# Attention scores of a fused transformer block: fp32 products against three fp32r passes on high and low parts

## The chip, the cores and the metric

One core of a Trainium2 chip runs the whole program: two model blocks in one launch, three mixers and three feed-forward networks, on 512 tokens of width 1024. The metric is the device time of that core in microseconds. TensorE is the matrix engine (PE in the profile, its weight loads PEld), VectorE is DVE, ScalarE is ACT, GpSimd is POOL, and SyncE issues most DMAs.

## The reference

Only the first mixer matters here, the dilated attention of `first_block`. There are 12 heads of 64, and every query looks at three dilated windows:

```python
q, k = rope(q, pos), rope(k, pos)
attn_out = dilated_attention(q, k, v).reshape(B, S, ATTN_WIDTH)

def dilated_branch(q, k, v, window, dilation):     # (128, 1), (512, 4), (2048, 16)
    ...
    s = jnp.einsum('brnqhd,brnkhd->brnhqk', qs.astype(jnp.float32), kb.astype(jnp.float32)) * scale
    s = jnp.where(valid[None, None, :, None], s, -jnp.inf)
    m = jnp.max(s, axis=-1, keepdims=True)
    e = jnp.exp(s - m)
    ...
    o = jnp.einsum('brnhqk,brnkhd->brnqhd', e / den, vb.astype(jnp.float32))
```

The kernel computes each causal score once per head and folds the three windows into one additive table (BIAS: 8 times the logarithm of the number of windows that see the key), so the scores of a head are 512 queries against the keys up to the query's block of 128. `rope` multiplies by cosines and adds the swapped halves times sines.

## The kernel before, in words

Activations lie transposed: features on the 128 partitions, 512 tokens along the row. Every projection is an output tile of 128 features, called a unit, and is computed as three fp32r passes: weights high times input high, high times low (line 394 and 395, `high_part`), and low times high (line 403, `low_part`). ScalarE makes the high part of the weights (a copy to fp32r, line 375), GpSimd the low part (weights minus high part, `split_lo`, line 647, both inputs in SBUF), and it starts on a unit as soon as the high part is there and the buffer's last unit has ended.

The attention takes the 12 heads as 6 pairs, one pair to a tile of 128 partitions: head h=0 on rows 0 to 63, head h=1 on rows 64 to 127. The code of each engine is a function `attn_stage(j, a)`: stage j projects queries, keys and values of pair j (units u, u+1, u+2) while it does scores, softmax and values of pair a = j - 1. The stages run j = 0 to 5, and then one with the last pair's attention alone. The order of each engine's work is written out by hand, and semaphores join the engines.

TensorE, stage j (lines 1033 to 1131): `scores` of pair a (line 1052); `turn_v` (1092); query unit into bank B[0]; `values` of pair a - 1 (1083); key unit into B[1]; `turn(0)`, ten transposes of head 0's probabilities (1068); a wait for the queries (`a_qk`, line 1128), since the value unit reuses B[0]; the high part of the value unit; `turn(1)`, which waits until VectorE has copied head 0's transposes out; its low part; in stages 2 and 4 one product of the pooling branch (1031). The next stage's `scores` wait for the keys (`a_qk`), and for both engines' copies of the turned probabilities (`a_pt_act`, `a_pt_dve`), because they reuse those banks.

The scores are 8 fp32 products, 4 per head, of widths 512, 384, 256 and 128 keys. Each contracts only 64 rows, so the two heads' products occupy different halves of the array. The profile shows an fp32 product as two matmul records, so 16 records per stage.

VectorE, stage j (2670 to 2775): `mask` and row maxima (2716), `normalise` (2725 to 2729), and for n = 0 (queries) and 1 (keys) `times_cos(n)` (2680), then, after ScalarE has copied the four swapped quarters (`swap_halves`, 1886), `rotate(n)`: times sine (2684), wait, and the add into QT1 or KT1 (2688, tiles QT and KT in the trace). In stages 2, 3 and 4 the window sums of the pooling branch (2650) stand between `rotate(0)` and `times_cos(1)`; stages 2 and 4 have its averages (2665) before `rotate(1)` and its differences (2668) after it. `copy_probs(0)` comes before `rotate(1)` and `copy_probs(1)` after it (2736, 2738); `scale_v` (2694) is last.

QT1 and KT1 are two buffers each in turns over the stages (index j % 2), fp32.

Of the kernel before, what the change touches and what calls it, by code (L numbers as in the profile page):

```python
# [19 lines left out]
P = 128  # L20
T = 512
D = 1024
DC = D // P
# [17 lines left out]
ALU = mybir.AluOpType  # L41
ACT = mybir.ActivationFunctionType
F32 = mybir.dt.float32
F32R = mybir.dt.float32r
# [43 lines left out]
def s_width(block):  # L88
    return P * (block + 1)
# [46 lines left out]
def build(nc, ins, out_t):  # L136
    ctx = ExitStack()
    with ctx:
# [6 lines left out]
        def sem(name):  # L145
            return ctx.enter_context(nc.semaphore(name))

        def scratch(tensors):

            with ExitStack() as stack:  # L150
                return [alloc(stack, *t) for t in tensors]
# [65 lines left out]
        def back(u):  # L217
# [3 lines left out]
        pad = 16  # L221
        (M1H, M1L, QT1, KT1, VN1, QC, RT, PR, PT, BIAS, CS1, SN1, V1, MX, NM, DEN, RD,
         UP, WA, WB, INV, DF, YT, WPOOL) = scratch([
             ("M1H", [P, DC, T], F32R), ("M1L", [P, DC, T], F32R), ("QT1", [P, 2, T]), ("KT1", [P, 2, T]),
             ("VN1", [P, 2, TB, P]), ("QC", [P, 2, T]), ("RT", [P, 2, T]), ("PR", [P, 2, WIDE]),
             ("PT", [P, 2, WIDE]), ("BIAS", [P, T]), ("CS1", [P, T]), ("SN1", [P, T]),
             ("V1", [P, T]), ("MX", [P, 2, TB]), ("NM", [P, 2, TB]), ("DEN", [P, 2, TB]), ("RD", [P, 2, TB]),
# [49 lines left out]
        B = [ctx.enter_context(nc.psum_tensor(f"B{n}", [P, T], F32)) for n in range(8)]  # L277
# [189 lines left out]
        a_cos = sem("a_qk_times_cosine")  # L467
        a_swapped = sem("a_qk_halves_swapped")
        a_sin = sem("a_qk_times_sine")
        a_qk = sem("a_qk_ready")  # L470
        a_vs = sem("a_v_scaled")
        a_vt = sem("a_v_turned")
        a_v = sem("a_v_ready")
        a_scores = sem("a_scores_ready")
# [234 lines left out]
        def _(pe):  # L709
# [323 lines left out]
            def attn_stage(j, a):  # L1033
# [4 lines left out]
                ap = None if a is None else a % 2  # L1038

                def scores():  # L1040

                    pe.wait_ge(a_qk, a * 2 + 2)
                    if not first_a:
                        pe.wait_ge(a_pt_act, a * 2)
                        pe.wait_ge(a_pt_dve, a * 4)
                    for h, tb, bank, at in ((0, 1, 4, 0), (1, 3, 5, 0), (0, 3, 2, 0), (1, 2, 6, 0), (0, 2, 3, 0),
                                            (1, 1, 4, 256), (0, 0, 3, 384), (1, 0, 6, 384)):
                        w = s_width(tb)
                        r = slice(64 * h, 64 * h + 64)
                        if h == 1 and bank == 4:  # L1050
                            pe.wait_ge(a_scores, a * 8 + 1)
                        pe.matmul(B[bank][:, at:at + w], QT1[r, ap, P * tb:P * tb + P], KT1[r, ap, 0:w],  # L1052
                                  start=True, stop=True).then_inc(a_scores, 1)

                def turn(h):
                    hd = a * 2 + h
# [38 lines left out]
                if a is not None:  # L1095
                    scores()
                    turn_v()
# [1083 lines left out]
        def _(dve):  # L2181
# [488 lines left out]
            def attn_stage(j, a):  # L2670
# [3 lines left out]
                jp = None if j is None else j % 2  # L2674
# [7 lines left out]
                def rotate(n):  # L2682
                    dve.wait_ge(a_swapped, j * 8 + 4 * n + 4)
                    dve.tensor_tensor(RT[:, 1, :], QC[:, n, :], SN1[:], ALU.mult).then_inc(a_sin, 1)
                    dve.wait_ge(a_sin, j * 2 + n + 1)
                    if j >= 2:
                        dve.wait_ge(a_scores, j * 8 - 8)
                    dve.tensor_tensor((QT1, KT1)[n][:, jp, :], RT[:, 0, :], RT[:, 1, :], ALU.add).then_inc(a_qk, 1)  # L2688

                def scale_v():  # L2690
                    wait_unit(dve, u + 2)
# [56 lines left out]
                if j is not None:  # L2748
                    rotate(0)
                    if a is not None and a - 1 in POOL_ENDS:  # L2750
                        pool_lo(POOL_ENDS[a - 1])
# [10 lines left out]
                if j is not None:  # L2762
                    if first:
                        take_pools()
                    if a in POOL_ENDS:
                        pool_averages(POOL_ENDS[a])
                    rotate(1)
                    if a in POOL_ENDS:
                        pool_differences(POOL_ENDS[a])
# [389 lines left out]
```

## Time and profile before

| | |
|---|---|
| median of 3 runs | 1915.99 us (1915.64 to 1916.06) |
| profiled execution, device time | 1915.55 us |
| its span, first to last instruction | 1913.8 us |
| mean granted TensorE clock | 1.000 |
| PE busy | 1907.8 us, 100% of the span |
| DVE busy | 1157.4 us, 60% |
| ACT busy | 886.8 us, 46% |
| POOL busy | 469.4 us, 25% |
| scores of the first mixer (line 1052) | 96 matmul records, from 37.5 to 159.4 us |

Busy time of an engine is the union of its instructions. A matmul's record is longer than the time it occupies the array, because consecutive ones overlap: the distance from one start to the next is what a matmul costs in a stream. A VectorE record overlaps the one before it by some 0.08 us where nothing holds it up.

### The profile page before, as it was taken

Reading aid. Unit: us, or ns where it says so; the run is one execution under the profiler, and the core shown is the slowest. Engines: PE = TensorE matmul, PEld = TensorE weight load, DVE = VectorE, ACT = ScalarE, POOL = GpSimd, SP = SyncE. Lnnn points to the kernel's source line nnn. Section 1 sums busy time; section 2 is a strip of 40 time slices with the busy share of each in tenths; the row PEclk is TensorE's granted clock in tenths of the full one; section 3 lists DMA queues with packets and bytes.
Section 4 is the critical chain, followed back from the end, with each engine's and each line's share of the span. In section 5 each row is a group of like instructions: output and inputs, shape, how many; then the busy total and the mean of one; then the engine's idle time right before and its main releaser. Section 6 shows DMA issues by size and latency. Waiting matters only on the chain.

```text
span 1913.8 us, 29035 instructions
## 1 busy us (share of the span) xinstructions
PE 1907.8 (100%) x10235; PEld 1617.4 (85%) x10235; DVE 1157.4 (60%) x1685; ACT 886.8 (46%) x1386; POOL 469.4 (25%) x181
## 2 busy tenths in 40 slices
PE   9999999999999999999999999999999999999999
PEld 6777889998888888888889999888777788999887
DVE  5775688866237455464277876423777778787500
ACT  6665544445234434434254444424767554444421
POOL 3323300003423343343420000443322240000243
PEclk9999999999999999999999999999999999999999
DMA  5222233223223232232333222332212132232232
GB/s 177 66 67 78 67 126 117 99 77 106 95 85 106 71 99 82 71 101 74 99 101 131 99 99 76 104 99 78 72 60 66 55 113 97 101 113 93 91 106 89
DMA packets 48889, 177.41 MB, mean 93 GB/s; under 512 B 5552, under 2 KB 6448, under 8 KB 48816
## 3 DMA queue, kind: packets, MB, share of 16 engines
q1 hardware_dynamic: 36864, 137.29, 22.1%
q10 hardware_dynamic: 11952, 39.13, 5.8%
q8 instruction: 47, 0.77, 0.2%
q14 instruction: 26, 0.21, 0.0%
HBM read 174.30 MB, written 2.10 MB: 92 GB/s over the span
## 4 chain that ended last, share of the span: by engine, by line
PE 98%; DVE 1%; ACT 0%; issue 0%; DMA 0%; SPq 0%; DVEq 0%; ACTq 0%
PE B L394 20%; PE B L395 20%; PE B L403 20%; PE B L870 6%; PE B L866 6%; PE B L868 6%; PE B L1224 1%; PE B L415 1%; PE B L1228 1%; PE B L1225 1%; PE B L420 1%; PE B L416 1%; PE B L1405 1%; PE B L1442 1%; PE B L1428 1%; PE B L1052 1%
## 5 line engine op out<-in xcount | busy, mean ns | idle before, releaser
L647 POOL TENSOR_TENSOR WL<-RAW,WH 128x1024 fp32r<-128x1024 f32 (+1 forms) x170 | 458.4, 2699 | 1418.9 <-ACT WH L375 854.8
L375 ACT CAST WH<-RAW 128x1024 fp32r<-128x1024 f32 (+1 forms) x232 | 258.4, 1115 | 444.1 <-PE B L395 358.2
L394 PE MATMUL B<-HH,WH 128*128 128x512 f32 x1064 | 418.9, 394 | 0.3 <-DVE QT L2688 0.3
L395 PE MATMUL B<-HL,WH 128*128 128x512 f32 x1064 | 415.4, 390 | 0.0
L403 PE MATMUL B<-HH,WL 128*128 128x512 f32 x1064 | 265.1, 391 | 0.0
L394 PEld LDWEIGHTS B<-HH,WH 128*128 128x128 f32 x1064 | 200.0, 188 | 42.2 <-issue 1.7
L395 PEld LDWEIGHTS B<-HL,WH 128*128 128x128 f32 x1064 | 200.1, 188 | 39.8
L403 PEld LDWEIGHTS B<-HH,WL 128*128 128x128 f32 x1064 | 196.8, 188 | 40.0 <-POOL WL L647 0.4
L395 PE MATMUL B<-ML,WH 128*128 128x512 f32 x440 | 171.3, 389 | 0.0
L394 PE MATMUL B<-MH,WH 128*128 128x512 f32 x440 | 171.3, 389 | 0.0
L870 PE MATMUL B<-TH,SL 128*128 128x256 f32 x544 | 153.0, 281 | 0.0
L866 PE MATMUL B<-TH,SH 128*128 128x256 f32 x544 | 153.0, 281 | 0.0
L868 PE MATMUL B<-TL,SH 128*128 128x256 f32 x544 | 152.9, 281 | 0.0
L1586 ACT CAST SH<-SUMS 128x512 fp32r<-128x512 f32 (+1 forms) x102 | 77.9, 765 | 135.5 <-DVE SUMS L2283 95.4
L2194 DVE TENSOR_TENSOR ACC<-ACC,SQ 128x512 f32<-128x512 f32 x38 | 74.6, 1964 | 107.9 <-ACT SQ L1531 107.8
L2474 DVE TENSOR_TENSOR X<-X,B 128x512 f32 x26 | 17.9, 687 | 198.8 <-PE B L403 193.2
L870 PE MATMUL B<-HH,SL 128*128 128x256 f32 x408 | 114.8, 281 | 0.0
L866 PE MATMUL B<-HH,SH 128*128 128x256 f32 x408 | 114.8, 281 | 0.0
L868 PE MATMUL B<-HL,SH 128*128 128x256 f32 x408 | 114.8, 281 | 0.0
L868 PEld LDWEIGHTS B<-TL,SH 128*128 128x128 f32 x544 | 104.3, 192 | 2.5
L866 PEld LDWEIGHTS B<-TH,SH 128*128 128x128 f32 x544 | 102.2, 188 | 2.6
L403 PE MATMUL B<-MH,WL 128*128 128x512 f32 x429 | 103.6, 389 | 0.0
(430 smaller groups left out, 3622.8 us busy)
## 6 DMA issues: line engine op xcount, KB each, us to landing
RAW<-in_w_small SPq DMA_DIRECT2D x186, 512.0 KB, 3.5
RAW<-in_w_large SPq DMA_DIRECT2D x48, 704.0 KB, 4.1
SUMS<-in_w_seven ACTq DMA_DIRECT2D x34, 512.0 KB, 3.6
R<-in_w_seven ACTq DMA_DIRECT2D x17, 512.0 KB, 4.4
HD<-in_w_seven ACTq DMA_DIRECT2D x17, 512.0 KB, 4.4
out_t<-X SPq DMA_DIRECT2D x7, 256.0 KB, 5.2
X<-in_x_t ACTq DMA_DIRECT2D x4, 256.0 KB, 6.3
X<-in_x_t SPq DMA_DIRECT2D x4, 256.0 KB, 6.6
```

The source lines that it names most:

```text
L375: act.copy(wh, raw).then_inc(s_hi, 1)
L394: pe.matmul(bank, wh[:, c, :], xh[:, k0 + c, :], start=(start and c == 0), stop=False)
L395: mm = pe.matmul(bank, wh[:, c, :], xl[:, k0 + c, :], start=False, stop=False)
L403: mm = pe.matmul(bank, wl[:, c, :], xh[:, k0 + c, :], start=False, stop=(stop and c == chunks - 1))
L415: pe.matmul(bank, wh[:, c, :], xh[:, k0 + c, :], start=(start and c == 0), stop=False)
L416: pe.matmul(bank, wh[:, c, :], xl[:, k0 + c, :], start=False, stop=False)
L647: pool.tensor_tensor(wl, raw, wh.bitcast(F32), ALU.subtract).then_inc(s_lo, 1)
L866: pe.matmul(bank, wh, xh[:, rows.start + c, cols], start=(start and c == 0), stop=False, skip_group_check=True)
L868: pe.matmul(bank, wh, xl[:, rows.start + c, cols], start=False, stop=False, skip_group_check=True)
L870: mm = pe.matmul(bank, wl, xh[:, rows.start + c, cols], start=False, stop=(c == 3), skip_group_check=True)
L1586: act.copy(SH7[:, form, :], src).then_inc(t_hi, 1)
L2194: dve.tensor_tensor(ACC[:], ACC[:], SQ[b][:], ALU.add).then_inc(s_sq_used, 1)
```

## The change

The scores are computed as three fp32r passes in place of fp32: query high times key high, query low times key high, query high times key low. The products are issued in four twos, one of each head, and within a two pass by pass. QT1 and KT1 become fp32r, and their two halves now hold the high and the low part of one pair in place of two pairs in turns, so that VectorE waits for all scores of the pair before (`a_scores`) before it writes them. `rotate(n)` gets two more VectorE operations: the add is done twice, once rounded to fp32r (the high part) and once in fp32 (into RT), and after a wait for both the difference is the low part.

```diff
-             ("M1H", [P, DC, T], F32R), ("M1L", [P, DC, T], F32R), ("QT1", [P, 2, T]), ("KT1", [P, 2, T]),
+             ("M1H", [P, DC, T], F32R), ("M1L", [P, DC, T], F32R), ("QT1", [P, 2, T], F32R), ("KT1", [P, 2, T], F32R),
...
-                    for h, tb, bank, at in ((0, 1, 4, 0), (1, 3, 5, 0), (0, 3, 2, 0), (1, 2, 6, 0), (0, 2, 3, 0),
-                                            (1, 1, 4, 256), (0, 0, 3, 384), (1, 0, 6, 384)):
-                        w = s_width(tb)
-                        r = slice(64 * h, 64 * h + 64)
-                        if h == 1 and bank == 4:
-                            pe.wait_ge(a_scores, a * 8 + 1)
-                        pe.matmul(B[bank][:, at:at + w], QT1[r, ap, P * tb:P * tb + P], KT1[r, ap, 0:w],
-                                  start=True, stop=True).then_inc(a_scores, 1)
+                    for two in (((0, 1, 4, 0), (1, 3, 5, 0)), ((0, 3, 2, 0), (1, 2, 6, 0)),
+                                ((0, 2, 3, 0), (1, 1, 4, 256)), ((0, 0, 3, 384), (1, 0, 6, 384))):
+                        for n, (q, k) in enumerate(((0, 0), (1, 0), (0, 1))):
+                            for h, tb, bank, at in two:
+                                w = s_width(tb)
+                                r = slice(64 * h, 64 * h + 64)
+                                if n == 0 and h == 1 and bank == 4:
+                                    pe.wait_ge(a_scores, a * 8 + 1)
+                                mm = pe.matmul(B[bank][:, at:at + w], QT1[r, q, P * tb:P * tb + P], KT1[r, k, 0:w],
+                                               start=(n == 0), stop=(n == 2), skip_group_check=True)
+                                if n == 2:
+                                    mm.then_inc(a_scores, 1)
...
-                    if j >= 2:
-                        dve.wait_ge(a_scores, j * 8 - 8)
-                    dve.tensor_tensor((QT1, KT1)[n][:, jp, :], RT[:, 0, :], RT[:, 1, :], ALU.add).then_inc(a_qk, 1)
+                    if j:
+                        dve.wait_ge(a_scores, j * 8)
+                    hi, lo = ((QT1, KT1)[n][:, part, :] for part in range(2))
+                    dve.tensor_tensor(hi, RT[:, 0, :], RT[:, 1, :], ALU.add).then_inc(a_hi, 1)
+                    dve.tensor_tensor(RT[:, 1, :], RT[:, 0, :], RT[:, 1, :], ALU.add).then_inc(a_hi, 1)
+                    dve.wait_ge(a_hi, j * 4 + 2 * n + 2)
+                    dve.tensor_tensor(lo, RT[:, 1, :], hi.bitcast(F32), ALU.subtract).then_inc(a_qk, 1)
```

## Rows read from the trace of the kernel before

**Rows 1.** The page, busy time (share of the span) xinstructions, and the chain by engine
```profile
PE 1907.8 (100%) x10235; PEld 1617.4 (85%) x10235; DVE 1157.4 (60%) x1685; ACT 886.8 (46%) x1386; POOL 469.4 (25%) x181
...
PE 98%; DVE 1%; ACT 0%; issue 0%; DMA 0%; SPq 0%; DVEq 0%; ACTq 0%
```

**Rows 2.** Waits of PE: who waited for whom, us in total, times, longest
```profile
PE B L394 <- DVE QT L2688: 0.3, 1, 0.3
```

**Rows 3.** Timeline of PE, first scores: start, us, instruction, count
```profile
37.51 2.43 PE L1052 MATMUL B<-KT,QT 64*128 64x256 f32 x16
39.87 0.66 PE L1092 MATMUL B<-IDENT,V 128*128 128x128 f32 x4
```

**Rows 4.** Timeline of PE, the fp32r scores of the second mixer, and what follows
```profile
623.06 0.39 PE L1320 MATMUL B<-QH,KH 128*128 128x512 f32 x1
...
626.87 0.40 PE L394 MATMUL B<-HH,WH 128*128 128x512 f32 x1
```

**Rows 5.** Timeline of DVE, the adds of stage 0
```profile
31.10 0.69 DVE L2688 TENSOR_TENSOR QT<-RT 128x512 f32<-128x512 f32 x1
...
35.77 0.69 DVE L2688 TENSOR_TENSOR KT<-RT 128x512 f32<-128x512 f32 x1
```

**Rows 6.** Timeline of POOL, six of its weight splits
```profile
31.68 2.41 POOL L647 TENSOR_TENSOR WL<-RAW,WH 128x1024 fp32r<-128x1024 f32 x1 [2.23 <-PE B L403]
...
51.53 2.45 POOL L647 TENSOR_TENSOR WL<-RAW,WH 128x1024 fp32r<-128x1024 f32 x1 [2.98 <-PE B L403]
...
100.58 2.40 POOL L647 TENSOR_TENSOR WL<-RAW,WH 128x1024 fp32r<-128x1024 f32 x1 [5.54 <-PE B L403]
108.36 2.35 POOL L647 TENSOR_TENSOR WL<-RAW,WH 128x1024 fp32r<-128x1024 f32 x1 [5.38 <-PE B L403]
...
455.64 6.07 POOL L647 TENSOR_TENSOR WL<-RAW,WH 128x1408 fp32r<-128x1408 f32 x1 [222.62 <-ACT WH L375]
...
617.87 2.82 POOL L647 TENSOR_TENSOR WL<-RAW,WH 128x1024 fp32r<-128x1024 f32 x1 [2.94 <-PE B L403]
```

**Rows 7.** Timeline of DVE beside the last two of these splits
```profile
452.52 6.10 DVE L2367 TENSOR_TENSOR ML<-HD,MH 128x512 fp32r<-128x512 f32 x10
...
617.74 3.49 DVE L2845 TENSOR_TENSOR KL<-KT,KH 128x512 fp32r<-128x512 f32 x2 [0.74 <-ACT KH L1984]
```

**Rows 8.** Timeline of DVE in stages 1, 2 and 3
```profile
51.05 0.69 DVE L2688 TENSOR_TENSOR QT<-RT 128x512 f32<-128x512 f32 x1
...
57.35 0.42 DVE L2738 COPY PT<-B 128x256 f32<-128x256 f32 x1
...
81.90 0.41 DVE L2738 COPY PT<-B 128x256 f32<-128x256 f32 x1
...
99.03 0.68 DVE L2650 TENSOR_TENSOR WA<-UP 128x512 f32<-128x512 f32 x1
99.75 0.69 DVE L2650 TENSOR_TENSOR WB<-WA 128x512 f32<-128x512 f32 x1
100.59 0.69 DVE L2680 TENSOR_TENSOR RT<-B,CS 128x512 f32<-128x512 f32 x1
...
106.42 0.41 DVE L2738 COPY PT<-B 128x256 f32<-128x256 f32 x1
```

**Rows 9.** Timeline of PE in stages 1 to 3 and at their ends
```profile
52.30 0.47 PE L394 MATMUL B<-HH,WH 128*128 128x512 f32 x1
...
59.08 2.43 PE L1052 MATMUL B<-KT,QT 64*128 64x256 f32 x16
...
84.04 0.70 PE L1052 MATMUL B<-KT,QT 64*128 64x256 f32 x3
...
105.11 1.25 PE L1068 MATMUL B<-IDENT,PR 128*128 128x128 f32 x10
...
108.14 1.13 PE L1052 MATMUL B<-KT,QT 64*128 64x256 f32 x5
```

**Rows 10.** Timeline of PE, its first six matmuls, fp32
```profile
1.32 5.49 PE L1156 MATMUL B<-RB 128*128 128x512 f32 x6 [1.32 <-POOL RB L650]
```

More of the change, by code:

```diff
@@ L469, in build @@
         a_sin = sem("a_qk_times_sine")
+        a_hi = sem("a_qk_high_and_sum")
         a_qk = sem("a_qk_ready")
```

## The prediction

> **What bounds the kernel now.** I read the page first: PE is busy 1907.8 of 1913.8 us and makes up 98% of the chain of waits [rows 1]. So a microsecond added to TensorE's own work, or to a wait of TensorE, is a microsecond of the kernel, and work on VectorE costs nothing while TensorE does not wait for it. The next view was the waits of PE. In the whole attention TensorE waits once for something that the change touches: 0.3 us in stage 0, for the queries [rows 2]. The third view was the timeline of all engines through one stage after another, to see how much slack stands in front of each wait that VectorE's added work can lengthen. There the reader should look at GpSimd too, for a reason below. The profiled execution took 1915.55 us; the median of the runs is 0.44 above it, and I add that at the end.
>
> **TensorE's part.** Today a stage's 16 records of scores occupy it from 37.51 until the transposes start at 39.87: 2.36 us for both heads [rows 3]. The new passes have their nearest rows in the second mixer, whose fp32r scores make, in 24 matmuls on the full array, six passes over the same widths 512, 384, 256 and 128: from 623.06 to 626.87, 3.81 us [rows 4]. Three passes of one head are therefore 1.90 us. If the two halves of the array run as they do now, both heads take 1.90 plus a start and a handover. Bounds on one side: with none of either, the gain is 0.46 us per stage; on the other, if the heads do not run side by side, both take 3.81 us and the loss is 1.45. I take 0.24 for start and handover, thus 2.14 and a gain of 0.22: six times that is -1.3 us. That the halves go on side by side I hold for likely, since the 64-row fp32 records do so now, but no row shows it for fp32r.
>
> The Trainium skill ("TensorE: Matmul & The Clock Gate", Part 3) says that matmuls start and end strictly in program order. With that, a head whose product is the narrower of a two waits for the other's pass, and going through the four twos at the intervals above I get about 0.1 us more per stage, so the sum would be 0.6 us higher. The row of 2.36 us is too close to either reading to decide.
>
> **VectorE's part.** `rotate` had one add; now it has a rounded add, an fp32 add that needs nothing new, and a subtraction that waits for both. Independent operations of this size follow each other at 0.61 us (ten in 6.10) [rows 7], dependent ones at 0.72 (99.03 to 99.75) [rows 8]. So `a_qk` comes 0.61 + 0.72 = 1.33 us later after each start, and each `rotate` holds VectorE 1.33 us longer: 12 of them, 16 us, nearly all beside TensorE's work. Rounding on the write costs nothing in rows 7. The earlier buffer reuse (wait for this stage's scores) costs nothing: those scores are the first thing in the stage and `rotate` comes ten microseconds later.
>
> **The port.** Now to GpSimd. All three operations of the new `rotate` read two SBUF inputs, and so does the weight split of GpSimd. Rows 6 and 7 show what happens when they meet: at 617.74 a pair of such operations on VectorE took 3.49 us in place of 1.3, because GpSimd's split came in at 617.87 and took until 620.69; the second ended 0.54 us behind it. A split that arrives while VectorE is in one operation gets in at a gap and holds the next until it ends. In one train of ten VectorE operations, all ready beforehand, it did not get in: there it was GpSimd that took 6.07 us (455.64). The new `rotate` is no such train: its subtraction waits for a semaphore first, and at that gap the split enters. So it matters in each stage where the six splits of rows 6 lie.
>
> Stage 0. The add starts at 31.10 [rows 5], a split is due at 31.68 [rows 6]. It enters before the second add or before the subtraction, with the same end: 34.1 + 0.54 for one operation and 0.72 for another, or about 35.4. Before, the queries were there at 31.79. That is 3.6 us later, and TensorE was already waiting, so all of it is on the path. The keys: they ended 4.67 us after the queries, will end 6.0 after, and TensorE asks for them 5.7 after (37.51 less 31.79): 0.3 more. Stage 0: +3.9.
>
> Stage 1. The add at 51.05 [rows 8], a split at 51.53 [rows 6]. The queries come at about 55.3. TensorE's value unit started at 52.30 [rows 9] with 0.5 us of slack: stall 3.0. Everything TensorE releases moves with it. The keys are in time, but `copy_probs(1)` stands behind `rotate(1)` on VectorE and ends near 62.2, and the next scores could start at 59.08 + 3.0: 0.15 more. Stage 1: +3.2.
>
> Stages 2 and 4 (alike). The query wait has over 3 us of slack. VectorE runs 1.33 late, makes up 0.7 in an idle gap before `times_cos(1)`, and adds 1.33 in `rotate(1)`: `copy_probs(1)` ended at 82.31 [rows 8], comes at 84.15 to 84.2, and the scores start at 84.04 [rows 9]. +0.13 each, +0.3 together.
>
> Stage 3. The window sums stood at 99.03 and 99.75 [rows 8], in front of the split of 100.58. Now the first starts at 100.36, the split comes during it and the second is held until 103.9. `times_cos(1)` moves from 100.59 to 103.95, 3.35 later. `copy_probs(0)` behind it ends at 105.6, and `turn(1)`, due at 105.11 [rows 9], waits 0.5. The subtraction of the keys would start at about 109.2; but the next split, due at 108.36 and with TensorE half a microsecond later at 108.9 [rows 6], stands ready 0.3 before. It holds the subtraction until about 112.05, `copy_probs(1)` ends at 113.0, and the scores that started at 108.14 [rows 9] start then. Stage 3: +4.9. If that second meeting is missed, by 0.3 us, it is +2.7.
>
> Stage 5 has a gap of 1.4 us on VectorE before `times_cos(1)`, no window sums, and no split near its rotations: nothing.
>
> Sum: 3.9 + 3.2 + 0.3 + 4.9 - 1.3 = +11.0 us on 1915.55, and with 0.44 for the median 1927.0. After the attention no wait of TensorE has slack to give anything back, since there is none to shorten.
>
> **Rivals.** First, not slower: VectorE keeps the port through `rotate`, as in the train at 452.52, and through the window sums. Then only plain lateness is left: 1.3 + 0.3 in stage 0, 0.8 + 0.2 in stage 1, 0.3 in stages 2 and 4, 0.6 in stage 3, together 3.6 against a gain of 1.3. That is +2.3, 1918.3, which is within 0.2% (3.8 us, about what a measurement can tell here from no change). It decides by whether the split enters at a semaphore wait; from a gain of 0.6 us per stage up it would even be faster, which takes more than the 0.46 of the bound above. Against it: the pair at 617.74. Chance 0.13, with 0.04 of it for faster than before by over 0.2% through a gain that I don't see.
>
> Second, the change does not do what it says: the two heads' fp32r passes run one after the other. Then each stage loses 1.45 in place of gaining 0.22, six times 1.67 is 10 us: 1937. The fp32 records of 64 rows speak against it; nothing shows it for fp32r. Chance 0.10.
>
> Third, TensorE's clock. It would stand still for about 3.9, 3.0 and 4.4 us, and the longest standstill before, in the first mixer, is 0.3 [rows 2], with the granted clock at full all along; whether it drops after such a stop no row says. What it costs can be read from the start: six fp32 records of 512 columns took 5.49 us [rows 10], 0.9 each, where today's scores come to 0.47 per 512 columns of a head (2.36 for two records of 1280 columns) [rows 3]. About half of 5.4 us would be lost per drop, 2.7 us. One or two drops: 1929.7 to 1932.4. The Trainium skill (the same page, Part 1) says that an idle TensorE falls back from 2.4 to 1.2 GHz, which makes this a case to reckon with, the longer the stop the more. Chance 0.15.
>
> **Numbers.** The forecast with its own variants (the second meeting in stage 3 missed, 1924.8; a split in stages 2 and 4 that slips in front of the window sum, which has only 0.15 us of room, 2 to 4 us more each) has 0.62. The range runs from the first rival to the third, 1918.5 to 1933. It leaves out the second rival and the far end of the first. Slower by over 0.2% 0.84, within 0.2% 0.12, faster 0.04.
>
> **What would show it.** The scores of a stage from first record to `turn_v`: 2.1 to 2.2 us if side by side, near 4 if not. In the waits of PE: one of about 3.9 us for QT in stage 0 and one of 3.0 in stage 1, before the value unit; waits before the scores of stages 0 to 4 for KT or for the copies PT. In the timeline of DVE: one of the three operations of `rotate(0)` at 2.5 to 3 us in stages 0 and 1, and the second window sum of stage 3 at nearly 3 us, each beginning within a split. If those take 0.69, the first rival holds. A granted clock below 1.00 right behind a stop would show the third. I am wrong altogether if TensorE waits nowhere, or if the loss lies outside 30 to 160 us.

## Result and the profile after

The changed kernel takes 1932.12 us (median of 4, 1931.07 to 1933.31) against 1916.03 (1915.64 to 1916.91). The ratio is 1.0084, 95% interval [1.0071, 1.0097]: 16.1 us slower, where 11.0 were forecast, and inside the range. The profiled execution took 1931.33 us, its span is 1929.5 and its mean granted clock 0.997; the two slowest of the four runs, 1932.92 and 1933.31, were granted 0.996.

The page, busy time and the chain of what ended last, beside [rows 1]:

```profile
PE 1910.1 (99%) x10283; PEld 1620.6 (84%) x10283; DVE 1179.2 (61%) x1709; ACT 886.7 (46%) x1386; POOL 470.5 (24%) x181
...
PE 95%; DVE 2%; ACT 1%; DMA 1%; issue 1%; ACTq 0%; SPq 0%; DVEq 0%
```

VectorE is busy 22 us more. That alone would cost nothing; what costs is in the waits of PE (us in total, times, longest), beside [rows 2]:

```profile
PE B L394 <- DVE QT L2697: 6.6, 2, 3.9
PE B L1055 <- DVE PT L2747: 4.1, 1, 4.1
PE B L867 <- ACT SQ L1659: 2.2, 2, 1.8
...
PE B L1073 <- DVE PT L2747: 0.4, 1, 0.4
```

Two stops for the queries (stages 0 and 1), one before the scores of stage 3 and a short one before its second transposes stand where the prediction put them. Of the two waits at line 867, one of 1.8 us is in the third feed-forward network, near 1620 (at the point that the kernel before reaches at 1606), and one of 0.4 in the first, near 306. Neither was foreseen. The timeline of DVE in stages 0, 1 and 3 shows why TensorE waits; 2694, 2695 and 2697 are the three operations of the new `rotate`:

```profile
30.88 0.69 DVE L2694 TENSOR_TENSOR QT<-RT 128x512 fp32r<-128x512 f32 x1
31.49 2.83 DVE L2695 TENSOR_TENSOR RT<-RT 128x512 f32<-128x512 f32 x1
34.35 0.69 DVE L2697 TENSOR_TENSOR QT<-RT,QT 128x512 fp32r<-128x512 f32 x1
...
56.21 2.83 DVE L2695 TENSOR_TENSOR RT<-RT 128x512 f32<-128x512 f32 x1
...
109.78 2.77 DVE L2655 TENSOR_TENSOR WB<-WA 128x512 f32<-128x512 f32 x1
...
117.79 2.73 DVE L2697 TENSOR_TENSOR KT<-RT,KT 128x512 fp32r<-128x512 f32 x1
```

Four operations of 0.69 us take 2.73 to 2.83. Each begins 0.1 to 0.5 us after one of these splits of POOL has begun and ends 0.5 us behind it, as the pair at 617.74 did [rows 6, 7]:

```profile
31.38 2.39 POOL L648 TENSOR_TENSOR WL<-RAW,WH 128x1024 fp32r<-128x1024 f32 x1 [2.14 <-PE B L403]
...
56.09 2.41 POOL L648 TENSOR_TENSOR WL<-RAW,WH 128x1024 fp32r<-128x1024 f32 x1 [2.98 <-PE B L403]
...
109.29 2.72 POOL L648 TENSOR_TENSOR WL<-RAW,WH 128x1024 fp32r<-128x1024 f32 x1 [5.53 <-PE B L403]
117.64 2.34 POOL L648 TENSOR_TENSOR WL<-RAW,WH 128x1024 fp32r<-128x1024 f32 x1 [5.63 <-PE B L403]
```

The busy time by stretch (length, then busy time and count of PE, PEld, DVE, ACT, POOL, granted clock, DMA) shows the second part of the loss: TensorE idle, and from the end of the stop (0.5 us before it to 0.7 behind it) 3.4 us at a granted clock of 0.50, its lower level of 1.2 GHz. There are three stops and three such stretches, the third through the scores of stage 3:

```profile
31.20:35.10 3.90, 0.03 (x1) 0.00 (x0) 3.81 (x3) 0.00 (x1) 2.39 (x1) 1.00 0.33 110
35.80:39.20 3.40, 3.40 (x10) 2.62 (x9) 2.11 (x5) 2.31 (x4) 0.00 (x0) 0.50 0.27 108
57.10:59.80 2.70, 0.00 (x0) 0.00 (x0) 2.64 (x2) 0.00 (x0) 1.40 (x1) 0.98 0.14 12
59.70:63.10 3.40, 3.27 (x8) 2.60 (x9) 1.78 (x5) 2.40 (x5) 0.00 (x0) 0.50 0.39 146
117.50:121.10 3.60, 0.00 (x0) 0.00 (x0) 3.57 (x4) 0.25 (x1) 2.34 (x1) 1.00 0.00 0
121.10:124.50 3.40, 2.90 (x18) 2.93 (x20) 1.35 (x4) 0.00 (x0) 0.00 (x0) 0.50 0.50 154
```

The scores themselves, in the timeline of PE beside [rows 3], stage 2, at full clock:

```profile
93.06 2.13 PE L1055 MATMUL B<-KT,QT 64*128 64x256 f32 x24
95.12 0.33 PE L1097 MATMUL B<-IDENT,V 128*128 128x128 f32 x1
```

They take 2.06 us from the first record to the transposes, where it was 2.36. In stage 3, at the lower level, they take 3.38:

```profile
121.60 3.45 PE L1055 MATMUL B<-KT,QT 64*128 64x256 f32 x24 [4.11 <-DVE PT L2747]
124.99 0.44 PE L1097 MATMUL B<-IDENT,V 128*128 128x128 f32 x2
```

**The sum, from the shift of the same TensorE instruction between the two traces.**

| place | forecast | measured |
|---|---|---|
| start of the program (TensorE comes to the first stop 0.25 earlier) | 0 | -0.25 |
| stage 0: stop for the queries, 31.84 to 35.10 | 3.6 | 3.5 |
| stage 0: lower clock behind it | 0 | 1.6 |
| stage 0: keys late for the scores | 0.3 | 0.0 |
| stage 1: stop for the queries, and before the scores | 3.2 | 3.0 |
| stage 1: lower clock | 0 | 1.5 |
| stages 2 and 4 | 0.3 | 0.4 |
| stage 3: wait at `turn(1)` and before the scores | 4.9 | 4.7 |
| stage 3: lower clock (scores in 3.38 in place of 2.07) | 0 | 1.3 |
| passes, six stages | -1.3 | -1.7 |
| behind the attention: the wait near 1606 of before, and smaller shifts that nearly cancel | 0 | 1.7 |
| sum | 11.0 | 15.7 |

15.7 is the difference of the two spans, within rounding. The start of the program is not the same in every trace: TensorE comes to stage 0 between 0.3 us earlier and 1.05 us later than in the trace of before, so a difference of a microsecond between two single executions says little.

### The profile page after: what moved, and what is told of

It is laid out like the page before. It is cut to its first block, busy times and chain, and to the rows that moved or that the text cites. A ratio compares the mean times of both kernels' runs of the same rounds, so it can differ in the third digit from the quotient of the medians.

```text
span 1929.5 us, 29157 instructions
## 1 busy us (share of the span) xinstructions
PE 1910.1 (99%) x10283; PEld 1620.6 (84%) x10283; DVE 1179.2 (61%) x1709; ACT 886.7 (46%) x1386; POOL 470.5 (24%) x181
## 4 chain that ended last, share of the span: by engine, by line
PE 95%; DVE 2%; ACT 1%; DMA 1%; issue 1%; ACTq 0%; SPq 0%; DVEq 0%
PE B L394 19%; PE B L395 19%; PE B L403 19%; PE B L871 6%; PE B L867 6%; PE B L869 6%; PE B L1229 1%; PE B L415 1%; PE B L1233 1%; PE B L1230 1%; PE B L416 1%; PE B L420 1%; PE B L1410 1%; PE B L1447 1%; PE B L1433 1%
```

## Experiments

All times are medians. The kernel before, run beside each of them, took 1915.6 to 1915.7.

**Each half alone.** First TensorE's (the diff is against the changed kernel; QT1 and KT1 are again two buffers in turns). All three passes work on the high parts and the low parts are left out, so the scores are less exact, but TensorE's work is the same:

```diff
-                                mm = pe.matmul(B[bank][:, at:at + w], QT1[r, q, P * tb:P * tb + P], KT1[r, k, 0:w],
+                                mm = pe.matmul(B[bank][:, at:at + w], QT1[r, ap, P * tb:P * tb + P], KT1[r, ap, 0:w],
...
-                    dve.tensor_tensor(RT[:, 1, :], RT[:, 0, :], RT[:, 1, :], ALU.add).then_inc(a_hi, 1)
-                    dve.wait_ge(a_hi, j * 4 + 2 * n + 2)
-                    dve.tensor_tensor(lo, RT[:, 1, :], hi.bitcast(F32), ALU.subtract).then_inc(a_qk, 1)
```

> TensorE's half alone: three fp32r passes per score product, but all three on the high parts (the low parts are left out of the computation), VectorE as in the kernel before, with one add per rotation. My theory: the passes run side by side and free 0.29 us per stage (2.07 in place of 2.36 from the first record to the transposes), no new wait: 1.7 us under the kernel before, 1914.3. Rival: the passes themselves or the fp32r form cost time elsewhere (clock, order): at or over the kernel before, 1916 or more.

1915.89 us (10 runs, 1914.0 to 1918.82), ratio 1.0000 [0.9991, 1.0010]. In the trace the attention is as expected: stage after stage takes 0.3 us less, and before the last transposes the program is 1.7 us ahead of before. But the median shows nothing of it. The waits of PE name the place:

```profile
PE B L866 <- ACT SQ L1658: 1.6, 1, 1.6
```

It is the wait that the changed kernel has near 1620. So the theory held for the attention and missed the total; I return to this wait below. Two of the ten runs took 1914.0 and 1914.57, less than any of the 19 of the kernel before (lowest 1915.09); they may be executions without this wait, but neither was traced.

Then VectorE's, with the scores of before (the diff is again against the changed kernel):

```diff
-             ("M1H", [P, DC, T], F32R), ("M1L", [P, DC, T], F32R), ("QT1", [P, 2, T], F32R), ("KT1", [P, 2, T], F32R),
+             ("M1H", [P, DC, T], F32R), ("M1L", [P, DC, T], F32R), ("QT1", [P, 2, T]), ("KT1", [P, 2, T]),
...
+                        pe.matmul(B[bank][:, at:at + w], QT1[r, 0, P * tb:P * tb + P], KT1[r, 0, 0:w],
+                                  start=True, stop=True).then_inc(a_scores, 1)
...
-                    dve.tensor_tensor(lo, RT[:, 1, :], hi.bitcast(F32), ALU.subtract).then_inc(a_qk, 1)
+                    dve.tensor_tensor(lo, RT[:, 1, :], hi, ALU.subtract).then_inc(a_qk, 1)
```

> VectorE's half alone: rounded add, second add, subtraction and their waits as in the changed kernel, but QT1 and KT1 stay fp32 and the scores are the old fp32 products of the first part. My theory: all of the loss is here. Stops of TensorE of about 3.9 us in stage 0, 2.7 in stage 1 and 4 in stage 3, three drops of the clock, and without the 1.7 us that the passes free: 1932.1 + 1.7 = 1933.8. Rival (the rounding to fp32r or the passes are what makes TensorE wait): well under 1932, near 1918.

1933.16 us (4 runs, 1930.05 to 1934.04). VectorE's half alone loses as much as both together, with the same waits of PE in the attention:

```profile
PE B L394 <- DVE QT L2693: 6.6, 2, 3.9
PE B L1053 <- DVE PT L2743: 4.1, 1, 4.1
```

The agreement with the forecast of 1933.8 is in part luck. The wait near 1606 is absent in this trace, and two of its three stretches of lower clock last 6.8 us in place of 3.4, those of stages 0 and 3. By the shift of TensorE's instructions the two cost 2.4 and 2.8 us, where the changed kernel's cost 1.6 and 1.3.

**The meetings taken away.** The four splits of GpSimd that met VectorE now wait for it: that of unit 5 for the queries of stage 0, that of unit 8 for the queries of stage 1, that of unit 14 for the key cosine of stage 3 and that of unit 15 for its keys:

```diff
-                    for n in range(2, 6):
-                        split_lo(Unit(n), chunks)
-                    start = 3
+                    guards = {5: (a_qk, 1), 8: (a_qk, 3), 14: (a_cos, 8), 15: (a_qk, 8)}
+                    for n in range(2, 16):
+                        if n in guards:
+                            pool.wait_ge(*guards[n])
+                        split_lo(Unit(n), chunks)
+                    start = 8
```

> The changed kernel, but four of GpSimd's weight splits (units 5, 8, 14, 15) wait until VectorE is through with the operations that they met: queries of stages 0 and 1, key cosine and keys of stage 3. Nothing else changes. My theory (the port makes the stops): all operations of rotate take 0.69 us, stops shrink to 1.3 + 0.3 in stage 0, 1.0 in stage 1, 0.6 in stage 3, the clock stays at full: 16.1 less 9 us of stops less 4.4 of clock, about 1918.3. Rival 1 (the operations are long for another reason, as rounding or the wait): still about 1932. Rival 2 (clock falls even after a stop of 1.3 us): about 1921.

1919.59 us (10 runs), ratio 1.0026 [1.0017, 1.0036]. The profiled execution has a granted clock of 1.000 from the first stop on. The waits of PE shrink to

```profile
PE B L394 <- DVE QT L2700: 2.0, 2, 1.4
...
PE B L870 <- ACT SQ L1662: 0.9, 1, 0.9
PE B L1058 <- DVE PT L2750: 0.6, 1, 0.6
PE B L1058 <- DVE KT L2700: 0.3, 1, 0.3
```

and on DVE the operation that took 2.83 is

```profile
32.29 0.68 DVE L2698 TENSOR_TENSOR RT<-RT 128x512 f32<-128x512 f32 x1
```

12.5 of the 16.1 us hang on when four GpSimd instructions start, though nothing on VectorE changed. (0.8 of them may be the wait near 1606, which is 0.9 us here and 1.8 in the changed kernel's trace.) Plain lateness (1.4 + 0.3 + 0.6 + 0.6) is what the first rival reckoned with. Most of the 1.3 us over my figure is in the figure: it took off 9 us of stops, and the measured 3.5, 3.0 and 4.7 less the 3.2 expected to remain are 8.0.

**The stops filled.** 15 and 12 needless matmuls before the wait for the queries, in stages 0 and 1:

```diff
+                    if j < 2:
+                        for n in range((15, 12)[j]):
+                            pe.matmul(B[(4, 7)[j]][:], HH[:, 0, 0:P], HH[:, 0, :], start=True, stop=True)
                     pe.wait_ge(a_qk, j * 2 + 1)
```

> The changed kernel with 15 and 12 needless matmuls of 512 columns into unused banks in stages 0 and 1, just before TensorE's wait for the queries; they fill most of the stop (3.4 of 3.9 us, 2.7 of 2.7). VectorE is untouched. My theory: the stop costs itself and, behind it, a clock at half; filled, the stops stay but two of three drops go: 1932.1 - 3.1 = 1929.0, PEclk 1.00 behind the first two, 0.5 only behind the one of stage 3. Rival (the half clock comes from the mix of instructions, not from the stop): no change, 1932; or the extra matmuls add to the time, 1933 and more.

1928.62 us (4 runs, 1928.03 to 1929.78). TensorE does 27 matmuls more and is 3.5 us faster. Stretches 30 to 70, then the end of the stop of stage 3 (116.0 to 120.2) and what follows:

```profile
30.00:44.00 14.00, 13.46 (x73) 10.80 (x71) 10.17 (x13) 5.67 (x9) 5.31 (x3) 1.00 0.22 75
44.00:70.00 26.00, 25.85 (x148) 21.40 (x145) 19.80 (x50) 14.44 (x31) 7.66 (x4) 1.00 0.20 62
...
118.30:125.10 6.80, 4.95 (x29) 4.86 (x30) 3.97 (x11) 0.09 (x1) 0.23 (x1) 0.50 0.24 80
```

The clock stays at full behind the filled stops and falls in the one left. So it is the standstill that brings the lower level. What that costs is best read within the attention. From the restart in stage 0 to `turn(1)` of stage 3 the changed kernel loses 6.0 us against before and this one 3.45: the two stretches of lower clock were worth about 2.5 us. The difference of the medians is a poor measure of it, since other things changed too: in this trace TensorE came to the first stop 1.3 us later than in the changed kernel's, the lower level of stage 3 lasted 6.8 us in place of 3.4 and cost 0.9 more, and there is no wait near 1606 at all.

**Stage 3 by itself.** Only the splits of units 5 and 8 wait (against the run in which four do):

```diff
-                    guards = {5: (a_qk, 1), 8: (a_qk, 3), 14: (a_cos, 8), 15: (a_qk, 8)}
+                    guards = {5: (a_qk, 1), 8: (a_qk, 3)}
```

> The changed kernel with only the splits of units 5 and 8 waiting (stages 0 and 1); those of stage 3 are left as they fall. My theory: the stops are independent. Stage 3 keeps 0.5 + 4.2 us less the 0.6 of plain lateness, and a drop of the clock behind it of 1.3 us: 5.5 over the run with all four splits waiting (1919.6), 1925.1. Rival (stage 3 is late because stages 0 and 1 were): near 1919.6.

1924.61 us (4 runs, 1923.43 to 1925.55). The stops are independent: stage 3's meetings and the lower clock that comes with them (6.8 us of it in this trace) are worth 5.0 us over the run with all four guarded.

```profile
PE B L1058 <- DVE PT L2750: 4.3, 2, 4.1
PE B L394 <- DVE QT L2700: 2.1, 2, 1.5
```

**The order of the matmuls.** Three passes of one product, then three of the next:

```diff
-                        for n, (q, k) in enumerate(((0, 0), (1, 0), (0, 1))):
-                            for h, tb, bank, at in two:
+                        for h, tb, bank, at in two:
+                            for n, (q, k) in enumerate(((0, 0), (1, 0), (0, 1))):
```

> The changed kernel, but the three passes of one product follow each other, then the three of the next, so that the heads change only every third matmul. If each half of the array takes its own next matmul (my reading of the rows of before), a stage's scores still take 2.07 us and the time stays at 1932. If matmuls start strictly in program order, the heads hardly overlap: over 3 us a stage, 6 us more, 1938.

1931.79 us (4 runs, 1930.27 to 1932.36), the same as the changed kernel, and the timeline of PE for the scores of stage 2 is the same too:

```profile
91.74 2.15 PE L1055 MATMUL B<-KT,QT 64*128 64x256 f32 x24
93.82 0.44 PE L1097 MATMUL B<-IDENT,V 128*128 128x128 f32 x2
```

That is 2.08 against 2.06 us. The starts of the single records say it directly: the first product of head 1 (512 wide), fourth in the program, starts at 91.75, and the second pass of head 0 (256 wide), second in the program, at 91.96. The two halves of the array each take their own next matmul, and the interleaving written into the change buys nothing. The strict order that the Trainium skill states ("TensorE: Matmul & The Clock Gate", Part 3) does not hold across row groups here. This trace also shows that a stop of 2.7 us need not bring the clock down: the one of stage 1 was followed by the full level, where the changed kernel's was followed by the half.

**A version with the stops taken out.** The sum goes into QC, the keys' cosine comes first, the queries' low part later, and bank 0 is free when it has been read:

```diff
-                    pe.wait_ge(a_qk, j * 2 + 1)
+                    pe.wait_ge(a_cos, j * 2 + 1)
+                    pe.wait_ge(a_swapped, j * 8 + 4)
...
-                    dve.tensor_tensor(RT[:, 1, :], RT[:, 0, :], RT[:, 1, :], ALU.add).then_inc(a_hi, 1)
+                    dve.tensor_tensor(QC[:, n, :], RT[:, 0, :], RT[:, 1, :], ALU.add).then_inc(a_hi, 1)
...
+                    low(0)
                     rotate(1)
+                    low(1)
...
+                    guards = {5: (a_hi, 2), 8: (a_hi, 6)}
```

> The changed kernel with its stops taken out as far as order allows: TensorE takes bank 0 again when VectorE and ScalarE have read it (cosine done, halves swapped), not when the queries are complete; the fp32 sum goes into QC, so that the key cosine comes before the queries' low part, which moves behind the copies and averages; and the splits of units 5 and 8 wait for the queries' sum. My theory, by going through the stages: 0.8 us of waiting left in stage 0, 0.3 each in stages 1, 2 and 4, 0.3 in 3, against 1.7 of gain: 0 to 0.5 us from the kernel before, about 1915.9, clock at full. Rival (the low parts are late wherever they stand): near the run with waiting splits, 1919.6.

1920.71 us (5 runs), where 1915.9 were expected. My going through the stages missed a meeting that the reordering itself made: TensorE, no longer held up in stage 0, released the next split (unit 6) at 37.39, where it starts at 39.64 in the run with four waiting splits, and so on top of the keys' low part. TensorE then waits 3.3 us before the scores, and 3.4 us at the lower clock follow. The wait, POOL and DVE:

```profile
PE B L1058 <- DVE KT L2704: 3.3, 1, 3.3
```

```profile
37.39 2.58 POOL L648 TENSOR_TENSOR WL<-RAW,WH 128x1024 fp32r<-128x1024 f32 x1 [2.40 <-PE B L403]
```

```profile
37.82 2.71 DVE L2704 TENSOR_TENSOR KT<-QC,KT 128x512 fp32r<-128x512 f32 x1
```

With that split held back as well:

```diff
-                    guards = {5: (a_hi, 2), 8: (a_hi, 6)}
+                    guards = {5: (a_hi, 2), 6: (a_qk, 2), 8: (a_hi, 6)}
```

> The reordered kernel once more, with one more split held back: that of unit 6 waits for the keys of stage 0, which it had met because TensorE came to it two microseconds earlier than before. My theory: the stop of 3.3 us before the first scores shrinks to 1.1, the clock keeps its level there (1.1 us), so 1920.7 - 3.3 = 1917.4, and up to 0.8 less where the late load near 1606 is not seen: at best level with the kernel before, never under it by 1 us. Rival (the stop was lateness, not a meeting): 1920.7.

1917.70 us (12 runs), ratio 1.0016 [1.0007, 1.0024]. The low part takes its own time again:

```profile
37.27 0.69 DVE L2704 TENSOR_TENSOR KT<-QC,KT 128x512 fp32r<-128x512 f32 x1
```

At the last scores (157.39 against 157.25) the attention is level with before, and 1.5 us is lost in the wait near 1606. No version that computes both parts beats the kernel before. Four of these 12 runs (1919.61 to 1924.44) were granted 0.998 or 0.999 on the mean; where the clock fell in them is not known, and one run of the kernel before (1919.54) was granted 0.999 too.

**The wait near 1606.** Two controls. The first is the kernel before with eight needless matmuls, so that everything behind stage 0 runs later:

```diff
+                    if j == 0:
+                        for _ in range(8):
+                            pe.matmul(B[4][:], HH[:, 0, 0:P], HH[:, 0, :], start=True, stop=True)
                     pe.wait_ge(a_qk, j * 2 + 1)
```

> The kernel before with eight needless matmuls in stage 0 (1.8 us, of which 0.3 fall into its one wait): everything behind runs 1.5 us later and nothing else changes. It asks where the 1.7 us went that the passes alone free in the attention and lose again at a load that lands late near 1606. If any shift of the program against the loads brings that wait: 1915.6 + 1.5 + up to 1.6 = 1918.7, and a wait of TensorE on ScalarE near 1608. If not: 1917.1 and no wait there.

1917.28 us (10 runs), no wait there. A shift of the program in time, 0.9 us at that point in this trace, does not bring it.

The second control is the kernel before without any edit.

> The kernel before, unchanged, for a second trace of it. If the late load near 1606 belongs to the chance of each execution, it can show here too; if it belongs to the changed kernels, TensorE has no wait there, as in the first trace. Time 1915.6 either way, 1.6 more with the late load.

1915.62 us, no wait there in the second trace either. So neither the chance of an execution nor a shift in time accounts for it, as far as three traces without it can say. What the traces with the wait share is in the view of the DMA, window 1596.4 to 1598.4 of the run with the passes alone (queue, packets, MB, share), and the loads of the network with their time to landing:

```profile
q8 instruction: 1, 0.02, 3.0%
...
SUMS<-in_w_seven ACTq DMA_DIRECT2D x1, 512.0 KB, 4.6
HD<-in_w_seven ACTq DMA_DIRECT2D x1, 512.0 KB, 6.7
```

In the kernel before the same two loads, window 1596 to 1610, land in

```profile
SUMS<-in_w_seven ACTq DMA_DIRECT2D x1, 512.0 KB, 3.5
HD<-in_w_seven ACTq DMA_DIRECT2D x1, 512.0 KB, 4.4
```

and the instruction fetch comes at 1607.7, behind them. The passes add 48 matmuls to TensorE's program, so its fetches lie elsewhere, and one lies on the start of these loads; HD comes 2.3 us later, VectorE and ScalarE after it, and TensorE waits 0.8 to 1.8 us, in each of the seven traces that have the passes and the fetch at this place (0.06 to 0.26 us before the issue of the load into HD). The run with the stops filled has its fetch 4.4 us before that issue, its load lands in 4.5 us, and TensorE does not wait there. The test was to lengthen the program at no cost to TensorE (the diff is against the run with the passes alone):

```diff
                     use_unit(pe, u + 1, B[1][:], DC, HH, HL)
+                    for _ in range(9):
+                        pe.wait_ge(s_warm, 1)
```

> TensorE's half alone, as in the first of these runs (all passes on the high parts), with nine more waits per stage on a semaphore long reached: 54 instructions that cost TensorE nothing and make its program longer. In the traces so far a 16 KB instruction fetch (queue 8) lies at 1598, right before the two weight loads of 1600 to 1605, wherever TensorE waits near 1606, and at 1607 or 1595 where it does not. My theory: with the longer program the fetch comes some 3 us earlier, the load is in time, and the 1.7 us freed in the attention reach the end: 1914.0, no wait near 1606. Rival (the wait comes with the passes whatever the program's length): 1915.9 again, wait of 1.6 us.

1915.41 us (11 runs), ratio 0.9996 [0.9987, 1.0005]. Near 1606 TensorE no longer waits: the fetch there is now 1.5 us before the issue of the load, where it was 0.2 (the 3 us of the expectation were too many), and the load lands in 4.5 us. But TensorE waits 1.6 us at 1011, at the same point of the second network, where no trace so far had a wait, and there a fetch now lies on the start of the loads (window 1000 to 1004):

```profile
PE B L866 <- ACT SQ L1660: 1.6, 1, 1.6
```

```profile
q8 instruction: 1, 0.02, 1.6%
...
SUMS<-in_w_seven ACTq DMA_DIRECT2D x1, 512.0 KB, 4.5
HD<-in_w_seven ACTq DMA_DIRECT2D x1, 512.0 KB, 6.6
```

> The reordered kernel with its three guarded splits, and the same 54 waits. My theory: 1917.7 less the 1.5 us near 1606: 1916.2, level with the kernel before. Rival: 1917.7 again.

The same addition to the reordered kernel: 1917.22 us (11 runs), ratio 1.0007 [0.9998, 1.0016], and again the wait near 1606 is gone and one of 1.7 us stands at 1013. Of the 54 added waits the two traces record 24 and 25 as instructions of their own. In time I was wrong both times, since the lost microsecond moved instead of going. For the cause the two runs say more than a success would: the wait follows the fetch. Over all 14 traces and the first HD load of each of the three networks, the nine loads with a fetch up to 0.3 us before their issue landed in 5.9 to 6.9 us, and 32 of the other 33 in 4.4 to 4.7. The one exception, 5.5 us in the first network of the changed kernel with no fetch near, makes the wait of 0.4 near 306, so a fetch is not the only thing that can make such a load late. A length that has neither wait, and would let the 1.7 us reach the end, was not tried.

## Why the prediction was right

The direction, the place and the mechanism were right, point by point. TensorE's part: the heads run side by side, in 2.07 us for a forecast 2.14; the passes free 1.7 us for 1.3, and the second rival is out. The strict-order variant is out too. VectorE's part: 1.33 us per rotation was forecast, and without meetings the stop of stage 0 is 1.4 us in all. The port: all four meetings that were named took place, at the operations named, with stops of 3.5, 3.0 and 4.7 us for 3.6, 3.2 and 4.9; that the second in stage 3 would be hit, by 0.3 us, held as well (by 0.15: the split begins at 117.64, the subtraction at 117.79). The first rival describes the kernel with the splits held back, and not the changed one; its terms add up to 3.5, where the prediction wrote 3.6.

One reason given for the meetings did not hold in general. The prediction let the split enter at the gap before the subtraction, which waits for a semaphore. In stages 0 and 1 the operation held up is the second add (line 2695), which waits for none: the first add ran from 30.88 to 31.57, the split began at 31.38, and the second add, begun at 31.49, was held. The sum allowed for either with the same end, so the time is not touched. Why the train of ten at 452.52 kept the split out and a train of two did not stays open.

Two terms were mis-sized. The sum had 0 for TensorE's clock, and its chance was put at 0.15; it fell at each of the three stops, 4.4 us together. The trace of before had no standstill over 0.8 us after its first matmul, so no row bore on it. The Trainium skill ("TensorE: Matmul & The Clock Gate", Part 1) says that an idle TensorE falls to the lower level. Here the traces agree with it: the granted clock fell to 0.50 at all nine stops of 3.3 to 4.1 us and at two of three of 2.7, and stayed at 1.00 behind all up to 1.8. The price per drop was put at 2.7 us, as half of the 5.4 us of the first six matmuls. In the changed kernel's trace each drop lasted 3.4 us and cost 1.3 to 1.6; where one lasted 6.8 us, as in three other traces, it cost 2.2 to 2.8. And the step "after the attention no wait of TensorE has slack to give anything back" stood in for "nothing happens there": the longer program put an instruction fetch on two weight loads, 1.7 us, as much as the passes had freed. Both were on the same side, hence 16.1 for 11.0. With its clock drops the changed kernel is in fact the third rival's case, and 1932.1 lies in that rival's 1929.7 to 1932.4; the forecast's own variants that reach as far, splits that slip in front of window sums in stages 2 and 4, did not occur. That the number fits so well is luck: the rival had one or two drops at 2.7 us, and what came was three at about 1.5 and a wait that nobody had forecast.

## What to carry to other kernels

VectorE work that seems hidden is to be laid over GpSimd's timeline before it is called free. Where both engines read two SBUF inputs, a 0.7 us operation of VectorE lasted 2.8, and making four GpSimd instructions wait for a semaphore gave back three quarters of the loss. (An operation with an input in PSUM, `times_cos` at 100.59 in [rows 8], took its 0.69 us within a split.) A new stop of TensorE is to be counted with the lower clock that may follow it: 11 of the 12 stops of 2.7 to 4.1 us in these traces brought it, at 1.3 to 2.8 us each. And a gain of one or two microseconds in one place is only had when the whole trace has been compared, since a program of another length can lose as much at an instruction fetch a millisecond later.

## What the runs showed of the hardware that was not expected

Halves of the array (64 rows each) take their matmuls independently of program order: 2.06 us interleaved pass by pass, 2.08 product by product. A split of GpSimd that comes in while VectorE is busy holds VectorE's next operation of this kind for 2.7 to 2.8 us in place of 0.69, even where that one waits for no semaphore; the split itself takes 2.34 to 2.72 us, where one alone takes 2.4. A 16 KB instruction fetch at the start of two 512 KB loads made the second land in 5.9 to 6.9 us in place of 4.4 to 4.7. How the one packet does this was not found. In those nine cases the load of the other queue (into RAW), issued 0.35 us after the one into HD as always, has its first packet 2.4 to 2.6 us after the issue of that one, in place of 3.6 to 4.0, so that the two run side by side for longer.
